# First feed-forward: u and g rows turned as 16-bit planes by DMA instead of by TensorE

## What is computed

```
def conv_glu(h, w_up, conv_w, conv_b, w_down):
    u, g = jnp.split(h @ w_up, 2, axis=-1)
    ...
    g = sum(gp[:, j:j + s_] * conv_w[j] for j in range(CONV_W)) + conv_b
    return (jax.nn.gelu(g, approximate=False) * u) @ w_down
```

## Time and profile before

| what | value |
|---|---|
| median of 3 runs | 2615.6 us (2615.4 to 2616.55) |
| the profiled execution, its own time | 2613.45 us |
| its span, first to last instruction | 2611.7 us |
| PE busy (matmul) | 2570.4 us, 98% |
| DVE busy | 1645.1 us, 63% |
| ACT busy | 1248.3 us, 48% |
| POOL busy | 221.2 us, 8% |
| DMA transposes (all in the second feed-forward) | 22 |
| granted TensorE clock, mean | 0.996 of full |

### The profile page before, as it was taken

The page is one execution under the profiler, slowest core; times in us unless marked ns, Lnnn a source line. Parts: engine busy times, 40 slices in busy tenths (PEclk is TensorE's granted clock), DMA queues, the critical chain, the costliest instruction groups (busy, mean ns, idle before and its releaser), DMA issues.

```text
span 2611.7 us, 32232 instructions
## 1 busy us (share of the span) xinstructions
PE 2570.4 (98%) x11706; PEld 2091.8 (80%) x11706; DVE 1645.1 (63%) x1827; ACT 1248.3 (48%) x1592; POOL 221.2 (8%) x269
## 2 busy tenths in 40 slices
PE   6999999999999999999999999999999999999998
PEld 2788888878888888888888877788888888888887
DVE  4987879977677666554554485756555555555444
ACT  3444456444444444444444465754455555554443
POOL 0030131300000000000100041301000000000000
PEclk8999999999999999999999999999999999999999
DMA  9997987967767666555676645466566767676664
GB/s 394 384 340 256 320 259 262 345 233 224 241 211 241 175 195 182 185 186 193 186 208 193 185 130 153 148 193 199 178 203 197 213 197 213 197 217 202 193 193 155
DMA packets 296399, 573.18 MB, mean 219 GB/s; under 512 B 47060, under 2 KB 47436, under 8 KB 295788
## 3 DMA queue, kind: packets, MB, share of 16 engines
q1 hardware_dynamic: 270352, 500.23, 60.1%
q0 software_dynamic: 18928, 69.39, 7.6%
q10 hardware_dynamic: 7020, 2.26, 0.6%
HBM read 563.94 MB, written 2.10 MB: 217 GB/s over the span
## 4 chain that ended last, share of the span: by engine, by line
PE 90%; DMA 4%; DVE 3%; issue 1%; ACT 1%; SPq 0%; POOL 0%; DVEq 0%; ACTq 0%
PE gp L1411 28%; PE gp L1413 28%; PE gp L1412 28%; DMA raw<-in_w_in_dram 2%; DMA proj<-in_w_ada_dram 1%; DVE w_lo L1917 1%; PE tp L1744 1%; DVE ada_sum L2044 1%; DMA ada_ring<-in_w_ada_dram 0%; PE tp L1487 0%; ACT w_hi L803 0%; PE tp L1652 0%; PE tp L1789 0%; PE tp L1642 0%; PE tp L1874 0%
## 5 line engine op out<-in xcount | busy, mean ns | idle before, releaser
L1917 DVE TENSOR_TENSOR w_lo<-raw,w_hi 128x1024 fp32r<-128x1024 f32 x872 | 1076.0, 1238 | 804.6 <-ACT w_hi L803 801.3
L803 ACT CAST w_hi<-raw 128x1024 fp32r<-128x1024 f32 x872 | 912.1, 1051 | 1041.6 <-PE gp L1413 890.1
L1411 PE MATMUL gp<-w_hi,h_hi 128*128 128x512 f32 x2656 | 1048.2, 395 | 6.8 <-DVE w_lo L1917 4.4
L1413 PE MATMUL gp<-w_hi,h_lo 128*128 128x512 f32 x2656 | 1035.6, 390 | 0.0
L1412 PE MATMUL gp<-w_lo,h_hi 128*128 128x512 f32 x2656 | 1035.1, 390 | 0.0
L1411 PEld LDWEIGHTS gp<-w_hi,h_hi 128*128 128x128 f32 x2656 | 499.4, 188 | 117.3 <-DVE w_lo L1917 9.8
L1413 PEld LDWEIGHTS gp<-w_hi,h_lo 128*128 128x128 f32 x2656 | 499.3, 188 | 105.4
L1412 PEld LDWEIGHTS gp<-w_lo,h_hi 128*128 128x128 f32 x2656 | 499.7, 188 | 101.3 <-issue 0.2
L1411 PE MATMUL gp<-w_hi,a_hi 128*128 128x512 f32 x704 | 274.6, 390 | 0.0
L1413 PE MATMUL gp<-w_hi,a_lo 128*128 128x512 f32 x704 | 273.9, 389 | 0.0
L1412 PE MATMUL gp<-w_lo,a_hi 128*128 128x512 f32 x704 | 273.9, 389 | 0.0
(11 more groups left out here) (313 smaller groups left out, 1364.9 us busy)
## 6 DMA issues: line engine op xcount, KB each, us to landing
raw<-in_w_in_dram SPq DMA_DIRECT2D x248, 512.0 KB, 4.5
raw<-in_w_up_dram SPq DMA_DIRECT2D x176, 512.0 KB, 4.2
raw<-in_w_ffn_in_dram SPq DMA_DIRECT2D x176, 512.0 KB, 4.3
ada_ring<-in_w_ada_dram POOLq DMA_DIRECT2D x128, 512.0 KB, 5.9
raw<-in_w_down_dram SPq DMA_DIRECT2D x88, 512.0 KB, 3.7
raw<-in_w_ffn_down_dram SPq DMA_DIRECT2D x88, 512.0 KB, 4.5
proj<-in_w_ada_dram SPq DMA_DIRECT2D x64, 512.0 KB, 10.4
raw<-in_w_out_dram SPq DMA_DIRECT2D x64, 512.0 KB, 4.8
```

The lines of the kernel that those rows point to most:

```text
L803: nc.scalar.copy(w_hi[:, s], raw[:, s]).then_inc(hi_ready, 1)
L1411: mm(o, hi[:, kt0 + kt, ps], w_hi[:, s, k, :], start=n == 0, stop=False)
L1413: return mm(o, lo[:, kt0 + kt, ps], w_hi[:, s, k, :], start=False, stop=n == g.kts - 1)
L1917: V.tensor_tensor(w_lo[:, s], raw[:, s], w_hi[:, s].bitcast(F32), ALU.subtract).then_inc(lo_ready, 1)
```

## The change

The first feed-forward takes the way of the second for both `u` and `g`. The drains write 16-bit planes straight from PSUM, so there is no step that splits planes. Two DMA transposes turn `u` (after block 7 of the pair's odd chunk), two turn `g` (after block 6 of the next even chunk), and ScalarE and VectorE join upper and lower halves. `u` waits in `u_rows`, which lies where `a_hi` of that pair will be, and once turned in `a_raw`, which lies where `a_lo` will be. The convolution reads `gt` in SBUF, no longer `tp`. The later steps move by one or two blocks: the first half of the convolution from block 5 to 7, its second half from block 6 to block 0 of the odd chunk, gelu from block 7 to 1 of the odd chunk, `times_u` from 0 to 2, the cast to `a_hi` from 1 to 3, `a_lo` from 2 to 4. SyncE's list for `g_up` and `g_down` is written out, where it was a loop. The core of the diff:

```
+            def turn_u(i):
+                for t in range(ST):
+                    sp.wait_ge(drained[t], g_up.chunk(i, 0) + 1)
+                if i:
+                    sp.wait_ge(ff_mul, i)
+                for t in range(ST):
+                    sp.dma_start_transpose(turned[:, :, t * P:(t + 1) * P],
+                                           u_planes(i, t).rearrange("p w n -> p (w n)")).then_inc(u_turned, 16)
+            def turn_g(i):
+                for t in range(ST):
+                    sp.wait_ge(drained[t], g_up.chunk(i, 1) + 1)
+                sp.wait_ge(u_joined, i * 2 + 2)
+                for t in range(ST):
+                    sp.dma_start_transpose(turned[:, :, t * P:(t + 1) * P],
+                                           g_planes(t).rearrange("p w n -> p (w n)")).then_inc(g_turned, 16)
+            def turn_up(i, e, j, first):
+                if e == 0 and not first and j == 6:
+                    turn_g(i - 1)
+                if e == 1 and j == 7:
+                    turn_u(i)
...
-                        nc.scalar.copy(ff[:, 0, t, :], gp[g_up.bank(e)][:, t, :]).then_inc(drained[t], 1)
+                        nc.scalar.copy(u_planes(i, t), bank_planes(g_up.bank(e), t)).then_inc(drained[t], 1)
+            def upper_u(i):
+                act.wait_ge(u_turned, i * 32 + 32)
+                nc.scalar.copy(a_half(i, 1), turned[:, 4:8, :]).then_inc(u_joined, 1)
+            def upper_g(i):
+                act.wait_ge(g_turned, i * 32 + 32)
+                nc.scalar.copy(g_half(1), turned[:, 4:8, :]).then_inc(g_joined, 1)
             def glu_each(i, e, j, first):
-                if e == 0 and not first and j == 7:
+                if e == 0 and not first and j == 1:
+                    upper_u(i - 1)
+                if e == 0 and not first and j == 6:
+                    upper_g(i - 1)
+                if later(i, e) and j == 1:
                     gelu(i - 1)
-                if later(i, e) and j == 1:
+                if later(i, e) and j == 3:
                     glu_parts(i - 1)
...
-            def pair_up(i):
-                for t in range(ST):
-                    pe.wait_ge(drained[t], g_up.chunk(i, 1) + 1)
-                for b in range(2):
-                    for f in range(4):
-                        for t in range(ST):
-                            o = (f % 2) * S + t * P
-                            last = nc.tensor.transpose(tp[:, 2 * b + f // 2, o:o + P],
-                                                       ff[:, b, t, f * P:(f + 1) * P], ident[:, :])
-                last.then_inc(ff_t, 1)
-            stream(g_up, h_hi, h_lo, 0, h_pairs(HB_NORM1), pair_up, each=rest_of_x)
+            stream(g_up, h_hi, h_lo, 0, h_pairs(HB_NORM1), each=rest_of_x)
...
-                        V.tensor_copy(ff[:, 1, t, :], gp[g_up.bank(e)][:, t, :]).then_inc(drained[t], 1)
+                        V.tensor_copy(g_planes(t), bank_planes(g_up.bank(e), t)).then_inc(drained[t], 1)
+            def lower_u(i):
+                dve.wait_ge(u_turned, i * 32 + 32)
+                V.tensor_copy(a_half(i, 0), turned[:, 0:4, :]).then_inc(u_joined, 1)
+            def lower_g(i):
+                dve.wait_ge(g_turned, i * 32 + 32)
+                V.tensor_copy(g_half(0), turned[:, 0:4, :]).then_inc(g_joined, 1)
...
             def conv_each(i, e, j, first):
-                if e == 0 and not first and j in (5, 6):
-                    conv(i - 1, j - 5)
+                if e == 0 and not first and j == 1:
+                    lower_u(i - 1)
+                if e == 0 and not first and j == 6:
+                    lower_g(i - 1)
+                if e == 0 and not first and j == 7:
+                    conv(i - 1, 0)
                 if later(i, e) and j == 0:
+                    conv(i - 1, 1)
+                if later(i, e) and j == 2:
                     times_u(i - 1)
-                if later(i, e) and j == 2:
+                if later(i, e) and j == 4:
                     glu_parts(i - 1)
```

More of the change, by code:

```diff
@@ L276, in two_blocks @@
         hf_ff = ff[:, 0].rearrange("p b (a s) -> p b a s", a=2)
-        g4 = ff[:, 1].rearrange("p t (a s) -> p (t a) s", a=2)
+        g4 = ff[:, 0].rearrange("p t (a s) -> p (t a) s", a=2)
+        gt = ff[:, 1].rearrange("p t (a s) -> p (t a) s", a=2)
         s2.close()
         s5 = ExitStack()
-        sb("under_a_raw", [P, FT * S], scope=s5)
+        u_rows = sb("u_rows", [P, FT, S], scope=s5)
         a_raw = sb("a_raw", [P, FT, S], scope=s5)
@@ L288, in two_blocks, with bank_planes, u_planes, g_planes @@
         planes_t = ff[:, 1].rearrange("p t n -> p (t n)").bitcast(U16).rearrange("p (q s) -> p q s", s=S)
+        turned = ff[:, 0].rearrange("p t n -> p (t n)").bitcast(U16).rearrange("p (q s) -> p q s", s=S)
+        def bank_planes(b, t):
+            return gp[b][:, t, :].bitcast(U16).rearrange("p (n w) -> p w n", w=2)
+        def u_planes(i, t):
+            return u_rows[:, bass.ds(i * 4 + 2 * t, 2), :].bitcast(U16)
+        def g_planes(t):
+            return ff[:, 1, t, :].bitcast(U16).rearrange("p (w n) -> p w n", w=2)
+        def g_half(w):
+            return gt.bitcast(U16).rearrange("p f (s w) -> p f s w", w=2)[:, :, :, w]
         def a_half(i, w):
@@ L403, in two_blocks @@
         ff_lo = sem("ff_lo")
+        u_turned = sem("u_turned")
+        u_joined = sem("u_joined")
+        g_turned = sem("g_turned")
+        g_joined = sem("g_joined")
         planes_ready = sem("planes_ready")
@@ L621, in turn, with turn_last_g @@
                                            planes[:, t].rearrange("p w n -> p (w n)")).then_inc(planes_turned, 16)
+            def turn_u(i):
[18 more added lines that the diff above has]
+                    turn_u(i)
+            def turn_last_g(i, e, j, first):
+                if first and j == 6:
+                    turn_g(g_up.chunks // 2 - 1)
             def turn_pair(i, e, j, first):
@@ L630, in _ @@
             for g, nxt in zip(gemms[1:], gemms[2:]):
-                stream(g, nxt, turn_pair if g is g_up2 else None)
+                stream(g, nxt, turn_up if g is g_up else turn_last_g if g is g_down
+                       else turn_pair if g is g_up2 else None)
             stream(g_down2, each=turn_last)
@@ L1170, in glu_parts @@
                 act.wait_ge(ff_mul, i + 1)
-                nc.scalar.copy(a_hi[:, bass.ds(i * 4, 4), :], g4).then_inc(ff_hi, 1)
+                nc.scalar.copy(a_hi[:, bass.ds(i * 4, 4), :], gt).then_inc(ff_hi, 1)
             act.preload_act_table(ACT.Gelu)
@@ L1186, in down_each @@
             def down_each(i, e, j, first):
-                if first and j == 7:
+                if first and j == 1:
+                    upper_u(g_up.chunks // 2 - 1)
+                if first and j == 6:
+                    upper_g(g_up.chunks // 2 - 1)
+                if first and j == 9:
                     gelu(g_up.chunks // 2 - 1)
-                if first and j == 9:
+                if first and j == 11:
                     glu_parts(g_up.chunks // 2 - 1)
@@ L1767, in down_each @@
             def down_each(i, e, j, first):
-                if first and j == 1:
-                    pair_up(g_up.chunks // 2 - 1)
                 if first and j == 8:
                     pe.wait_ge(ada_summed, ADA_N)
-                    pe.wait_ge(ff_mul, g_up.chunks // 2)
                     sum_broadcast(gate2, lambda q: tp[:, q, :]).then_inc(mod_sum, 1)
@@ L2374, in conv @@
                 fs, n0 = (2 * half, 2 * half + 1), 6 * half
-                dve.wait_ge(ff_t, i + 1)
+                dve.wait_ge(g_joined, i * 2 + 2)
                 for f in fs:
@@ L2397, in times_u @@
                 dve.wait_ge(ff_act, i + 1)
[L2398 removed]
+                V.tensor_tensor(gt, g4, a_raw[:, bass.ds(i * 4, 4), :], ALU.mult).then_inc(ff_mul, 1)
             def glu_parts(i):
                 dve.wait_ge(ff_hi, i + 1)
[L2402 removed]
+                V.tensor_tensor(a_lo[:, bass.ds(i * 4, 4), :], gt, a_hi[:, bass.ds(i * 4, 4), :].bitcast(F32),
                                 ALU.subtract).then_inc(ff_lo, 1)
@@ L2440, in down_each @@
                 last_pair = g_up.chunks // 2 - 1
-                if first and j in (5, 6):
-                    conv(last_pair, j - 5)
-                if first and j == 8:
+                if first and j == 1:
+                    lower_u(last_pair)
+                if first and j == 6:
+                    lower_g(last_pair)
+                if first and j in (7, 8):
+                    conv(last_pair, j - 7)
+                if first and j == 10:
                     times_u(last_pair)
-                if first and j == 10:
+                if first and j == 12:
                     glu_parts(last_pair)
-                if first and j == 12:
                     dve.wait_ge(mod_sum, 6)
```

5 lines of the change are left out of this document (removed).

## The result

| | before | after |
|---|---|---|
| median, runs of one chip | 2615.98 us (2615.4 to 2620.41, 6 runs) | 2599.73 us (2595.45 to 2604.99, 6 runs) |
| ratio | | 0.9934, 95% interval 0.9923 to 0.9946 |
| profiled execution, and its span | 2613.45, 2611.7 us | 2595.45, 2593.7 us |

The change makes the kernel faster by 17.3 us by the ratio (14.1 to 20.1 by its interval); the two medians lie 16.3 us apart. The forecast was 19.5 us less and 2596.1. The time is 3.6 us above that point: above the forecast's own range, 2594.5 to 2598, and within the wider one, 2594.2 to 2604, that takes in rival 1. The profile after, first the page: busy time by engine, and two of its costliest groups.

The account below looks back on a forecast made before the run. PE was taken to bound the first feed-forward; removing its transposes saves 1.77 x 11 = 19.5 us with nothing back, so 2615.6 - 19.5 = 2596.1 us. Own range 2594.5 to 2598, wider range 2594.2 to 2604; forecast 80%.

Parts of the forecast that it names:

- rival 1: Up product: late steps make PE wait about 1 us in each of six pairs, 6 to 8 us back, 2604; 11%.
- What bounds the kernel: First feed-forward: PE, busy all 407.70 us of the stretch, sets the pace, and its 176 transposes are part of it.
- The 19.5 us: Up product and start of down product: removing 16 transposes from PE saves 1.77 us in each of 11 pairs.
- the spread of before: Whole kernel: the runs' spread of 1.2 us was used for the forecast's own range, 2594.5 to 2598.
- Costs on the other engines: Per pair: VectorE +1.8 us, ScalarE +3.7, SyncE 5.1 for four transposes; none on PE, so nothing back.
- The step-by-step times of a pair: Fullest up-product pair, followed from T, PE's start of the even chunk: each split is done before PE wants its block.
- The margin: Split of block 9 in a pair with modulation products: done 2.9 us before PE wants it, the pair's least.
- takes SyncE to 28.9, and the next load leaves 0.5 us later: Turn of u behind block 15's load: SyncE done at T + 28.9, next load 0.5 us late, some 2 us in hand.
- Landings above 4 us: Sign of a wrong forecast: DMA transposes landing after more than 4 us, where 2.8 was expected.
- Rival 2: Up product: something other than PE paces the pair at 45.3 us, so no change, 2615.6; 4%.
- Rival 3: Transposes of g land late, up to 10.4 us, on crowded DMA engines; PE waits 30 us, slower at 2626; 4%.
- Rival 4: Tiles of g go one by one, 1.27 us apart; 9.7 us lost per pair, slower at 2703; 1%.

Follow-up runs that it names:

- b1: New kernel with 16 unused transposes per pair put back on PE at the old place; 2616.96 us, ratio to before 1.001.
- f2: New kernel with the turn of u moved from behind block 7 to behind block 5 in all pairs; 2598.17 us, ratio to before 0.9926.
- a1: The new kernel unaltered, measured again on another occasion; 2599.05 us, ratio to before 0.9935.
- e4: New kernel with two more DMA transposes ahead of the two of g in each of the first ten pairs; 2605.02 us, ratio to before 0.9952.
- d1: New kernel with SyncE waiting until block 15's weight load has landed before it issues the turn of u; 2601.53 us, ratio to before 0.9949.

## Why the prediction was right, and where it was off

- **What bounds the kernel: right.** PE's list alone sets the up product. With the transposes back (b1) a pair takes 45.29 us and without them 43.52; with half of them 44.45.
- **The 19.5 us: right.** Measured from the start of the up product to the end of the program it is 19.7 (17.4 + 2.3) in an execution in which nothing came back. The ratio's interval, 14.1 to 20.1 us, holds it. The median is 3.6 above the point: 0.4 because before's own was 2615.98 in this comparison; the rest fits executions with a late first mark (f2) or a disturbed first pair (a1), though which of the two held up the three executions over 2602 us of the first comparison their times alone don't tell. I had put the spread of before, 1.2 us in three runs, on the new kernel; it was 9 us in six. That was the term taken too small, and before itself ranged over 2613.2 to 2623.7 in the later sets. By it the median left the forecast's own range. That the time still lies in the wider range is in part luck, since that room was made for rival 1, waits in six pairs around the split of block 9, and no profile of the new kernel shows these.
- **Costs on the other engines.** Drains of `g` 1.21 us (1.22 taken), drains of `u` 1.01 (1.05 taken; so ScalarE is quicker than VectorE at this PSUM read), joins 0.75 and 1.36 as taken. The first steps of the convolution went from 0.54 to 0.41, not to 0.35: the row I took had a different tile. Worth 0.2 us a pair, hidden. SyncE's four transposes take 7.8 us of the pair below, not 5.1. VectorE is busy 34.2 to 35.1 us in each of the three pairs from 622.84 on, not up to 38: the average that I added four products to held most of them already.
- **The step-by-step times of a pair: right to 0.3 us.** For the pair whose block 3 is cast at 666.56, T is 666.36. Rows of SyncE, ScalarE and VectorE there, the turn of `g`, its join, the cast of block 7, and the split of block 9:

```profile
671.21 2.59 SPq L657 DMA_TRANSPOSE ff<-ff  x2
```
```profile
675.67 1.35 ACT L1213 COPY ff<-ff 128x1024 uint16<-128x1024 uint16 x1
677.82 1.05 ACT L851 CAST w_hi<-raw 128x1024 fp32r<-128x1024 f32 x1 [0.79 <-DMA raw<-in_w_up_dram]
```
```profile
686.92 1.22 DVE L1968 TENSOR_TENSOR w_lo<-raw,w_hi 128x1024 fp32r<-128x1024 f32 x1
```

  Turn at T + 4.85 (4.75), join at 9.3 (9.35), cast of block 7 at 11.5 (11.6), split 9 done at 688.14 = T + 21.8 (21.55). The margin is 2.7, not 2.9, and e4 shows that it is real and that it is the least one.
- **The step that failed: the turn of u "takes SyncE to 28.9, and the next load leaves 0.5 us later".** I had taken the issue and landing of the second feed-forward's transposes. But for `g` the load in front has left 4.0 us before (667.17, the turn at 671.21), nearly what a load takes to land in the median, 4.5, while this one is issued 0.1 us behind load 15 (693.13, 693.24). In the pair above SyncE is at it from 693.24 for 5.23 us, to T + 32.1, and the landing is 5.9. The next load leaves at 698.52, 3.5 us after the split that frees its slot (block 12, done at 695.0), not 0.5. It cost nothing in most pairs: the first cast behind it starts 0.7 us late (702.64 against T + 35.6) and PE has more in hand than that. In the first pair, where the DMA engines are full, the up product of a1 is 5.8 us longer, and no other pair of it has a wait of PE. "Landings above 4 us" was one of my signs for wrong; it came, and the gain held, so the sign was too strict for `u`, whose join is due 16 us later.
- **Rival 1** (waits of PE give part back) is the near miss: in the first profile no pair loses, in a1 the first one does, though not by the path that the rival named, as it is a load behind the turn of `u` that comes late. **Rival 2** (no change) is out by the result and by b1. **Rival 3** (late landings of `g`) did not come: 2.8 in the median, 4.8 at most. **Rival 4** (tiles one by one) did not come either. The rule of the Trainium skill, "VectorE: DVE Perf Modes" (Rules for kernel authors), to transpose 128 x 128 on TensorE if PSUM will do as destination, does not agree with this case: 16 tiles cost PE 1.77 us, eight tiles in one DMA transpose land in 2.8 us beside other work, and time is won by taking them off the engine that bounds.

## What to carry to other kernels

When one engine is busy the whole time, cost its list by the distance between two equal steps with and without the item, and for all that goes elsewhere follow one full pair step by step until the least margin is found: here that was right to 0.3 us for `g` and named the block where a further delay showed up first. Take the price of a DMA from a row with the same traffic in front of it; an issue that stands right behind a load on its own queue is a different one. And compare spans cut at marks that both kernels have, since the part ahead of the first mark, which was not changed, moved by up to 7.6 us between executions.

## What was not expected of the hardware

- A DMA transpose of 128 x 1024 halves issued directly behind a 512 KB weight load in flight on SyncE's queue took 2.0 us of SyncE (up to 4.2) and landed in 5.9 us; with that load landed, 1.3 and 2.8 (d1). The modulation loads on GpSimd's queue are not the reason: the turns of `u` in the last pairs, after these have ended, take SyncE as long (two in 5.08 us at 953.29).
- The same turn of `u` in the same place of the first pair left the load behind it to land in some 6 us in one execution and in 11 in another (the first profile and a1); in the 5 us behind it the DMA engines, about as busy in both (1.12 and 1.19), moved 375 and 140 GB/s.
- After a pause of 4.07 us PE ran its next matmuls 0.43 us apart, not 0.227: 1.2 GHz, not 2.4, over six steps, which added 1.5 us to the wait itself (a1). After its pauses of 1.3 to 1.5 us in e4 the granted clock stays at 1.00 in the 10 us that follow.
